# Two heads per transpose for the latent keys, the rope key as eight fp32 products, and a reordered opening

## The reference

```python
def mla_expand(c_kv, k_rope, w_kvup, qk_k_norm):
    kv = (c_kv @ w_kvup).reshape(B, K, 8, 64 + 64)          # 8 heads: 64 plain key dims, 64 value dims
    k_nope, v = kv[..., :64], kv[..., 64:]
    kr = jnp.broadcast_to(k_rope[:, :, None, :], (B, K, 8, 32))   # 32 rope dims, shared by the heads
    return rmsnorm(jnp.concatenate([k_nope, kr], axis=-1), qk_k_norm), v
# in a layer
h = rmsnorm(x, norm_mix); proj = h @ w_in                   # q latent 384, kv latent 256, rope key 32, ...
c_kv = rmsnorm(kv_lat, mla_kv_norm); k_rope = apply_rope(kr_raw, pos)
km, vm = mla_expand(concat(past latents, c_kv), concat(past rope keys, k_rope), ...)
ym = mla_attend(qm, km, vm, ...)                            # chunk-causal softmax(q k / sqrt(96)) v
```

## Time and profile before

| | us |
|---|---|
| median of 3 runs | 1072.66 (1070.98 to 1074.01) |
| the profiled execution | 1072.71 |
| its span | 1070.9 |

### The profile page before, as it was taken

How to read it: one execution, slowest core, us unless ns; L and a number is a source line. 1 busy time by engine, 2 the same in 40 slices (tenths; PEclk the granted TensorE clock), 3 DMA queues, 4 the chain that set the end, 5 groups by cost and what they waited for, 6 DMA issues and landing times.

```text
span 1070.9 us, 19944 instructions
## 1 busy us (share of the span) xinstructions
PE 1056.9 (99%) x7558; PEld 1020.8 (95%) x7558; DVE 632.9 (59%) x1047; ACT 507.0 (47%) x895; POOL 312.7 (29%) x230
## 2 busy tenths in 40 slices
PE   8899999999999999999999999999999999999998
PEld 6889988999999999999989999889999999999998
DVE  5659655445666665643566795544457666556444
ACT  6455745444454434334454466444445443443332
POOL 1655454651121111100124645565312111110000
PEclk9999999999999999999999999999999999999999
DMA  6446333324444444445413444332345354444443
GB/s 229 117 119 180 125 117 101 110 92 152 142 136 159 159 153 151 143 162 168 158 65 135 137 131 125 118 101 96 121 146 167 115 168 151 156 139 155 158 142 123
DMA packets 48769, 147.90 MB, mean 138 GB/s; under 512 B 8480, under 2 KB 13952, under 8 KB 48704
## 3 DMA queue, kind: packets, MB, share of 16 engines
q1 hardware_dynamic: 41552, 142.79, 41.5%
q10 hardware_dynamic: 7152, 4.20, 1.3%
HBM read 143.75 MB, written 3.22 MB: 137 GB/s over the span
## 4 chain that ended last, share of the span: by engine, by line
PE 93%; DVE 4%; ACT 1%; POOL 1%; issue 0%; ACTq 0%; POOLq 0%; DVEq 0%
PE psum L479 28%; PE psum L480 27%; PE psum L481 27%; PE psum L642 1%; PE psum L603 1%; PE psum L634 1%; PE psum L626 1%; PE psum L567 1%; POOL ssum L1731 1%; PE psum L570 1%; PE psum L568 1%; PE psum L587 1%; PE psum L588 1%; PE psum L674 0%; PE psum L590 0%; PE psum L846 0%
## 5 line engine op out<-in xcount | busy, mean ns | idle before, releaser
L479 PE MATMUL psum<-AH,WH 128*128 128x320 f32 x1344 | 421.1, 313 | 1.2 <-DVE krt L1537 0.7
L481 PE MATMUL psum<-AH,WL 128*128 128x320 f32 x1344 | 415.3, 309 | 0.0
L480 PE MATMUL psum<-AL,WH 128*128 128x320 f32 x1344 | 415.2, 309 | 0.0
L479 PEld LDWEIGHTS psum<-AH,WH 128*128 128x128 f32 x1344 | 252.3, 188 | 6.5 <-issue 4.2
L480 PEld LDWEIGHTS psum<-AL,WH 128*128 128x128 f32 x1344 | 252.4, 188 | 0.9
L481 PEld LDWEIGHTS psum<-AH,WL 128*128 128x128 f32 x1344 | 252.3, 188 | 0.0
L922 ACT CAST WH<-raw 128x1024 fp32r<-128x1024 f32 x175 | 182.6, 1046 | 138.5 <-PE psum L481 136.8
L1736 POOL TENSOR_TENSOR WL<-raw,WH 128x1024 fp32r<-128x1024 f32 x71 | 174.0, 2461 | 167.1 <-ACT WH L922 167.1
L1305 DVE TENSOR_TENSOR WL<-raw,WH 128x1024 fp32r<-128x1024 f32 x102 | 126.3, 1239 | 116.9 <-ACT WH L922 116.7
L1490 DVE TENSOR_TENSOR WL<-raw,WH 128x1024 fp32r<-128x1024 f32 x88 | 107.6, 1223 | 49.6 <-ACT WH L1073 48.2
L1741 POOL TENSOR_TENSOR fab<-fa,fb 128x320 f32<-128x320 f32 x44 | 38.7, 879 | 270.1 <-DVE fb L1495 270.1
(11 more groups left out here) (239 smaller groups left out, 1556.7 us busy)
## 6 DMA issues: line engine op xcount, KB each, us to landing
raw<-w_all SPq DMA_DIRECT2D x267, 512.0 KB, 3.5
y_out<-X SPq DMA_DIRECT2D x8, 160.0 KB, 3.0
ckv<-lat_in ACTq DMA_DIRECT2D x2, 384.0 KB, 5.4
X<-x_in ACTq DMA_DIRECT2D x2, 320.0 KB, 8.5
X<-x_in ACTq DMA_DIRECT2D x1, 640.0 KB, 10.4
lat_out<-ckv ACTq DMA_DIRECT2D x2, 320.0 KB, 4.3
scratch<-brel SPq DMA_DIRECT2D x8, 63.8 KB, 4.1
bias<-scratch SPq DMA_DIRECT2D x8, 48.0 KB, 4.2
```

The lines of the kernel that those rows point to most:

```text
L479: mm(out, WH[:, slot, c0:c0 + cols], high, start=first, stop=False)
L480: mm(out, WH[:, slot, c0:c0 + cols], low, start=False, stop=False)
L481: return mm(out, WL[:, slot, c0:c0 + cols], high, start=False, stop=last)
```

## The change

1. `Kn` holds all plain columns (8 x 64) first and then all rope columns (8 x 32). A block is turned in six transposes: four of two heads each, two of four heads' rope rows each. `key_columns` moves them in three instructions per engine (plain rows of the even heads and rope rows of two groups on ScalarE, the rest on VectorE), and both `kt_act` and `kt_dve` are awaited before the first transpose of the next block.
2. The rope key is computed by eight fp32 matmuls of 64 weight columns, straight from x and a weight scaled by the norm's gain on VectorE (`WF`), even chunks into PSUM rows 0 to 63 and odd chunks into 64 to 127. ScalarE copies one half out (`rope_half`), VectorE adds the two and scales.
3. The first key and value products wait for the high half alone, the last two matmuls of the group for the low one.
4. Opening: `WARM` 7; the first weight unit is loaded in two halves by two engines; the table load stands ahead of the last four of ScalarE's loads; in layer 0 ScalarE rounds the first latent unit ahead of the key blocks, casts two chunks of x already between the first block's key square and its value copy, and the second latent unit in block 2; the unit `U_KR` isn't rounded any more, and `U_QL`, `U_QL + 1` and `U_QL + 2` each come one place earlier; GpSimd splits its unit and sums the first squares earlier.
5. The splits of the units `U_QL + 1`, `U_QL + 2` and `U_POOL` go from GpSimd to VectorE. `low(l, U_KR)` on VectorE gives way to `WF`. In layer 0 the latent's sum goes into the middle of the unit `U_QL + 1`.
6. `prompt()` of item 5 is issued before the values of item 4, `sample()` after them.

```diff
-WARM = 4
+WARM = 7
...
+    rW = base[0]
     WH = sb("WH", [128, RING, 1024], F32R)
+    WF = at("WF", [128, KC, 64], F32, rW + U_KR % RING * 4096)
...
-        sp.dma_start(raw[:, 0, :], w_all[stored(0)]).then_inc(raw_ready[0], 16)
+        sp.dma_start(raw[:, 0, 0:512], w_all[stored(0)][:, 0:512]).then_inc(raw_ready[0], 16)
...
+        def rope_columns(l):
+
+            open_tile(l, T_KR)
+            pe.wait_ge(s.split_ready, l * NU + U_KR + 1)
+            for k in range(KC):
+                half = slice(k % 2 * 64, k % 2 * 64 + 64)
+                last = mm(psum[half, tbank(T_KR), 0:T], WF[:, k, :], X[:, k, :], start=k < 2, stop=k >= KC - 2)
+            last.then_inc(s.tile_full, 1)
...
             if kb == 0:
-                pe.wait_ge(s.split_ready, l * NU + U_KVK + 1)
+                pe.wait_ge(s.high_ready, l * NU + U_KVK + 1)
...
+            if kb == 0:
+                pe.wait_ge(s.split_ready, l * NU + U_KVK + 1)
             for c in range(2):
                 last = mm(out, ckvH[:, c, keys], wl[:, c], start=False, stop=c == 1)
             last.then_inc(s.kn_full, 1)
...
-            for h in range(MH):
-                if kb > 0 and h % 4 == 0:
-                    if h == 0:
-                        pe.wait_ge(s.kt_act, l * KB + kb)
-                    else:
-                        pe.wait_ge(s.kt_dve, l * KB + kb)
-                last = nc.tensor.transpose(psum[0:QK, h // 4, (h % 4) * 128:(h % 4) * 128 + 128],
-                                           Kn[:, kb % 2, h, :], ident)
-                if h % 4 == 3:
+            if kb > 0:
+                pe.wait_ge(s.kt_act, l * KB + kb)
+                pe.wait_ge(s.kt_dve, l * KB + kb)
+            for c in range(6):
+                last = nc.tensor.transpose(psum[:, c // 4, (c % 4) * 128:(c % 4) * 128 + 128],
+                                           Kn[:, kb % 2, c * 128:c * 128 + 128], ident)
+                if c in (3, 5):
                     last.then_inc(s.kt_full, 1)
...
             if i == SW_ITEMS:
-                prompt()
+                if part == 0:
+                    prompt()
+                    return
                 pe.wait_ge(s.tile_free, l * NT + item_tile(SW_ITEMS - 1) + 1)
                 last = sample()
...
-            dense(l, U_KR, T_KR)
+            rope_columns(l)
...
-                if i + 1 < SW_ITEMS:
-                    scores(l, i + 1)
+                scores(l, i + 1)
                 values(l, i)
 
             for j in range(4):
                 i = SW_ITEMS + j
-                scores(l, i)
+                scores(l, i, part=1)
...
+        def rope_half(l):
+
+            act.wait_ge(s.tile_full, l * NT + T_KR + 1)
+            nc.scalar.copy(krt[64:128, 1, :], psum[0:64, tbank(T_KR), 0:T]).then_inc(s.kr_half, 1)
...
+        def cached_first(l):
 
             lat = lat_in[ds(l, 1)].rearrange("a p c n -> (a p) c n")
             act.dma_start(ckv[:, :, T:T + 128], lat[:, :, 0:128]).then_inc(s.cache_lat[0], 16)
+            if l == 0:
+                act.dma_start(raw[:, 0, 512:1024], w_all[stored(0)][:, 512:1024]).then_inc(s.half_in, 16)
             act.dma_start(krT[64:96, T:NKEY], kr_in[ds(l, 1)].rearrange("a p n -> (a p) n")).then_inc(s.cache_kr, 16)
+
+        def cached_rest(l):
+
+            lat = lat_in[ds(l, 1)].rearrange("a p c n -> (a p) c n")
             act.dma_start(ckv[:, :, T + 128:NKEY], lat[:, :, 128:PAST]).then_inc(s.cache_lat[1], 16)
...
-            A(Kt[0:QK, 0:4, KEY0[kb]:KEY0[kb] + n],
-              psum[0:QK, 0, :].rearrange("p (h n) -> p h n", h=4)[:, :, 0:n], ACT.Copy,
-              scale=kgain[0:QK]).then_inc(s.kt_act, 1)
+            keys = slice(KEY0[kb], KEY0[kb] + n)
+            A(Kt[0:NOPE, 0:MH:2, keys], psum[0:64, 0, :].rearrange("p (h n) -> p h n", h=4)[:, :, 0:n], ACT.Copy,
+              scale=kgain[0:64, 0:1])
+            act.wait_ge(s.kt_full, 2 * (l * KB + kb) + 2)
+            for r in range(2):
+                rows = slice(r * 32, r * 32 + 32)
+                ins = A(Kt[NOPE:QK, r:MH:4, keys], psum[rows, 1, 0:256].rearrange("p (h n) -> p h n", h=2)[:, :, 0:n],
+                        ACT.Copy, scale=kgain[rows, 1:2])
+            ins.then_inc(s.kt_act, 1)
...
-        cached_latent(0)
+        cached_first(0)
+        act.wait_ge(s.warm_zero, 1)
+        A(small[:, 31:32], ssum[:, 0:1], ACT.Sqrt)
+        cached_rest(0)
         act.dma_start(X[:, 0:2, :], x_in[:, 0:2, :]).then_inc(s.x_in[0], 16)
         act.dma_start(X[:, 2:4, :], x_in[:, 2:4, :]).then_inc(s.x_in[1], 16)
         act.dma_start(X[:, 4:8, :], x_in[:, 4:8, :]).then_inc(s.x_in[2], 16)
-        act.wait_ge(s.warm_zero, 1)
-        A(small[:, 31:32], ssum[:, 0:1], ACT.Sqrt)
         cached_high(0, 0)
+        act.wait_ge(s.half_in, 16)
         high(0, U_KVK)
         high(0, U_KVV)
         cached_high(0, 1)
+        high(0, U_KV)
...
+            keys = slice(KEY0[kb], KEY0[kb] + n)
+            dve.wait_ge(s.kt_full, 2 * (l * KB + kb) + 1)
+            v.tensor_scalar(Kt[0:NOPE, 1:MH:2, keys], psum[64:128, 0, :].rearrange("p (h n) -> p h n", h=4)[:, :, 0:n],
+                            kgain[64:128, 0:1], None, ALU.mult)
             dve.wait_ge(s.kt_full, 2 * (l * KB + kb) + 2)
-            v.tensor_scalar(Kt[0:QK, 4:8, KEY0[kb]:KEY0[kb] + n],
-                            psum[0:QK, 1, :].rearrange("p (h n) -> p h n", h=4)[:, :, 0:n],
-                            kgain[0:QK], None, ALU.mult).then_inc(s.kt_dve, 1)
+            for r in range(2, 4):
+                rows = slice(r * 32, r * 32 + 32)
+                ins = v.tensor_scalar(Kt[NOPE:QK, r:MH:4, keys],
+                                      psum[rows, 1, 0:256].rearrange("p (h n) -> p h n", h=2)[:, :, 0:n],
+                                      kgain[rows, 1:2], None, ALU.mult)
+            ins.then_inc(s.kt_dve, 1)
 
...
-            low(l, U_KR)
+            dve.wait_ge(raw_ready[U_KR % RING], (l * (NU // RING) + U_KR // RING + 1) * 16)
+            TT(WF[:], raw[:, U_KR % RING, :].rearrange("p (k c) -> p k c", k=KC)[:, :, 0:64],
+               col(C_MIX, l, n=KC)[:, :, None].to_broadcast([128, KC, 64]), ALU.mult).then_inc(s.split_ready, 1)
             low(l, U_QL)
+            low(l, U_QL + 1)
             stream_rstd(l, 0)
             scaled(l, T_KV, kvr[:, 0, :])
             scaled(l, T_KV + 1, kvr[:, 1, :])
+            low(l, U_QL + 2)
 
             dve.wait_ge(s.cst_in, 32)
 
             p = full_tile(l, T_KR)
-            TT(krt[64:128, 0, :], p[64:128, 0:T], rstd[64:128], ALU.mult).then_inc(s.tile_free, 1)
+            dve.wait_ge(s.kr_half, l + 1)
+            TT(krt[64:128, 0, :], p[64:128, 0:T], krt[64:128, 1, :], ALU.add).then_inc(s.tile_free, 1)
             dve.wait_ge(s.tile_free, l * NT + T_KR + 1)
+            link(l, TT(krt[64:128, 0, :], krt[64:128, 0, :], rstd[64:128], ALU.mult))
             TT(krt[64:96, 1, :], krt[64:96, 0, :], tab[64:96], ALU.mult)
             link(l, TT(krt[64:96, 2, :], krt[96:128, 0, :], tab[96:128], ALU.mult))
             TT(krT[64:96, 0:T], krt[64:96, 1, :], krt[64:96, 2, :], ALU.add).then_inc(s.kr_ready, 1)
             scaled(l, T_QL, qlr[:, 0, :])
-            if l == 0:
-                scaled(l, T_QL + 1, qlr[:, 1, :])
             r = recip(l, N_KV, 128, T)
             STT(ckv[:, 0, 0:T], kvr[:, 0, :], col(C_MKV, l), r, ALU.mult, ALU.mult)
             STT(ckv[:, 1, 0:T], kvr[:, 1, :], col(C_MKV + 1, l), r, ALU.mult, ALU.mult).then_inc(s.stat_applied, 1)
-            if l > 0:
-                scaled(l, T_QL + 1, qlr[:, 1, :])
+            scaled(l, T_QL + 1, qlr[:, 1, :])
             dve.wait_ge(s.ckv_high, l + 1)
             TT(ckvL[:, :, 0:T], ckv[:, :, 0:T], ckvH[:, :, 0:T].bitcast(F32), ALU.subtract).then_inc(s.ckv_ready, 1)
+            low(l, U_POOL)
```

More of the change, by code:

```diff
@@ L497, in dense, with latent_sum @@
             for k in range(KC):
+                if k == KC // 2 and between is not None:
+                    between()
                 last = products(out, u % RING, k * 128, 128, AH[:, k, :], AL[:, k, :], k == 0, k == KC - 1)
             last.then_inc(s.tile_full, 1)
+        def latent_sum(l):
+            b = stat_bank(l, N_KV + 1)
+            pe.wait_ge(s.sq_kv, l + 1)
+            for m in range(2):
+                last = mm(psum[:, b, 0:T], ones, SQ[:, m, :], start=m == 0, stop=m == 1)
+            last.then_inc(s.stat_full, 1)
         def two_dense(l, u, banks, ah, al, ready, value, done, between=None, cuts=(0, KC - 1, KC),
@@ L1117, in _ @@
             if l == 0:
-                for k in range(4):
-                    norm_chunk(l, 0, k, high=False)
                 act.wait_ge(s.x_in[2], 16)
@@ L1508, in _ @@
             dve.wait_ge(s.par_in, 16)
[L1509 removed]
+            dims, turn = slice(0, NOPE), slice(NOPE, QK)
+            for c in range(2):
+                TT(kgain[c * 64:c * 64 + 64, 0:1], col(C_GK, l, dims), col(C_GQ, l, dims), ALU.mult)
+            for r in range(4):
```

(2 more changed lines are left out.)

97 lines of the change are left out of this document (51 added, 46 removed).

## The result

| | us | ratio to before (95%) |
|---|---|---|
| before, median of 15 runs | 1072.67 (1070.79 to 1075.61) | |
| after, median of 15 runs | 1075.82 (1074.43 to 1077.36) | 1.0032 (1.0024 to 1.0039) |

The change costs 3.4 us by the ratio (3.2 by the medians), where 5.4 us of gain were forecast. The profiled execution of the changed kernel took 1077.36 us for a span of 1075.6: it is the longest of the 15, with a mean clock of 0.995.

The account below looks back on a forecast made before the run. TensorE was taken as the bound, busy 1056.9 of 1070.9 us. Layer 0 at -6.2, layer 1 at +0.3 and the scores at +0.5 summed to -5.4, so 1067.3 us, with a range of 1062.3 to 1071.0.

Parts of the forecast that it names:

- Layer 0, opening: Layer 0's start: TensorE starts at 7.9 us, first transposes at 15.8 against 16.42; layer 0 in all -6.2 us.
- the third rival: TensorE's clock falls after waits: one to three falls give 1069.0 to 1072.4 us, from the fourth 1074.1; chance 0.15.
- the doubled gains ... cost nothing beyond this walk: All layers: moved splits, doubled gains and divided first load add no time beyond the steps already priced.
- The key columns: Key blocks: three instructions per engine instead of one cost VectorE 0.95 us more per block, ScalarE about 0.75.
- the walk of layer 1: Layer 1's key blocks along VectorE: latent products end 2.1 us later; with rope and later blocks, +0.3 us.
- The rope key: Rope key in both layers: eight fp32 matmuls on column halves take 2.4 us instead of 3.60, 1.2 less per layer.
- "Layer 0", from the rope products to the new keys: Layer 0's middle: rope products end at 36.4 us, new keys start at 50.0 instead of 54.27, without a slow stretch.
- Prompt scores ahead: Last window item: a wait of 0.85 us becomes 1.1 before the sample scores; +0.3 per layer, +0.5 in all.
- its first rival: VectorE's key column price is hidden: layer 1 gives -2.8 us, the opening 1.3 more, 1062.9 us; chance 0.25.

Follow-up runs that it names:

- old_loads: Changed kernel with the opening's loads in the order of the kernel before (first weight unit whole, table load last): 1072.39 us, ratio 0.9996.
- eight_keys: Changed kernel with the eight transposes, one key column instruction per engine and single gain of before: 1067.10 us, ratio 0.9948.
- longer_warm: Changed kernel with ten warm matmuls instead of seven: 1074.90 us, ratio 1.0020.
- gains_early: Changed kernel with layer 0's six gains computed earlier, before VectorE's split of the remaining latents: 1073.81 us, ratio 1.0006.
- loads_and_gains: Changed kernel with the edits of both old_loads and gains_early: 1071.58 us, ratio 0.9992.
- eight_old_loads: Changed kernel with the eight transposes, key columns and single gain of before, and the opening's loads as before: 1064.71 us, ratio 0.9924.
- three_on_vector: eight_old_loads with VectorE's 96x512 key columns cut into 64x512 and two of 32x256: 1068.28 us, ratio 0.9956.
- three_on_scalar: eight_old_loads with ScalarE's 96x512 key columns cut into three pieces, VectorE's left whole: 1066.57 us, ratio 0.9938.
- middle_only: Kernel before with only the halved rope key, the splits moved to VectorE with their casts, and the moved latent sum: 1066.80 us, ratio 0.9947.
- rope_only: Kernel before with only the rope key on column halves: 1075.86 us, ratio 1.0024.
- one_split_on_gpsimd: eight_old_loads with the split of the third query unit back on GpSimd in both layers: 1063.60 us, ratio 0.9917.

## Why the prediction was wrong

**The failed step: "Layer 0, opening", to the first transposes.** The forecast had TensorE start at 7.9, the remaining latents at 10 and the first transposes at 15.8. They came at 9.60, 12.53 and 19.91. I put the lateness of that load down to its issue, "some 1.9 us later", 1.28 of it for the table load, "behind another 256 KB". The 8.52 of the earlier trace rows and 1.9 are 10.4 already, so the 10 left nothing for the 256 KB. The trace has it the other way round. The issue came only 0.58 us later, about the length of the one more issue, with the table load beside it, and the time from issue to landing grew from 6.4 to 9.8 us. It was 8.0 to 9.8 in the five traces with the new loads and 6.3 to 7.5 in the fifteen with the old ones. What in the new order slows the transfer stays open: the half unit now stands ahead of the latents in ScalarE's issues, and no run takes it back alone. Behind the load come ScalarE's moved cast and the first square, at 14.21 instead of my 11.75. old_loads puts 3.9 us on all this. The small load of the first latents, issued at 0.74 as before, is no such case. Its cast came at 7.72 here but at 5.03 in eight_keys with the same loads, against 5.74 to 6.99 in the traces with the kernel before's opening. The prediction had named loads after 11 us as what would make it wrong.

The clock fell three times up to the new keys of the profiled execution, twice before, as the third rival said; in the median it weighs little. The ground against that rival, that only waits over 2.5 us were followed by a fall, does not hold in this trace: one fall came behind a wait of 2.07 and one behind three short ones, while a wait of 2.44 in longer_warm had none.

**"... the doubled gains ... cost nothing beyond this walk"** is the second failed statement. Two operands in SBUF, a GpSimd split beside them, and one gain of 0.15 us took 2.27, with the first reduction behind it. That is 2.8 us in gains_early (1.4 by the trace of the changed kernel), and 0.4 with the old loads, which isn't told from nothing.

**"The key columns" and the walk of layer 1: right in kind, too small.** 1.24 us more per block on VectorE instead of 0.95 (I had bounds of 0.65 and 1.45). TensorE's waits were 1.43, 1.76 and 0.58 for my 0.9, 1.8 and 0.4; the latent products of layer 1 ended 2.8 us late instead of 2.1, and the later blocks gave 0.17 back instead of 0.6, since the next set waited for VectorE again. In layer 0 I had the period at 4.4 and then let the stream's second half end where it did; the trace adds 1.4 us of waits for low halves that VectorE makes after the late columns. Three of these four took 1.12 to 1.17 us instead of 0.54, beside GpSimd's additions for the sum of squares, which the walk had at nothing too:

```profile
34.51 3.75 DVE L1371 SCALAR_TENSOR_TENSOR AL<-X,par,AH 128x320 fp32r<-128x320 f32 x4
```

In all the six transposes cost 7.3 us (loads_and_gains against eight_old_loads), about 4.8 of it before layer 1 starts (540.27 against 535.43; of this, 0.6 is there at the first transposes already, 16.45 against 15.81). three_on_vector and three_on_scalar are 3.4 and 1.5: they don't add up to it. What is left, 2.4 us and what TensorE saves in the transposes, may be the 0.24 per block and the rule that the first transpose waits for both engines, where before the first four needed ScalarE alone; this is argued, and the two were not separated.

**"The rope key": right on TensorE** (2.31 us from start to start for my 2.4), and worth about 1.4 in the end for the 2.4 of both layers: in layer 0 VectorE sets the start of the new keys.

**"Layer 0", from the rope products to the new keys: right.** 15.9 us forecast, 42.22 to 58.18 measured, no clock of 0.50 behind the wait of 0.58. middle_only shows this alone: 5.7 us faster than before. I didn't see why it works. I priced the moved splits as time on GpSimd and VectorE, and rope_only shows that leaving them makes VectorE wait.

**"Prompt scores ahead", +0.5:** the wait of 0.83 is gone and one of 1.05 stands before the sample scores, as forecast; the sum can't be told from nothing.

The four differences, in the order before, middle_only, eight_old_loads, loads_and_gains, changed kernel: -5.7 for the middle, -2.5 for the rest of the opening and the scores (intervals that overlap by a hair), +7.3 for the six transposes, +4.3 for loads and gains. As a chain from the one kernel to the other they must add up to the measured +3.4, so the sum is no check; each difference is one measurement. By an estimate from its own terms the forecast had the six transposes at 1.6 (4.4 for VectorE's work by its first rival, less 2.8 saved), loads and gains at nothing, and so the first two at -7.0 together. The side was wrong because late loads and held gains in the opening were priced at a part or at zero, and because the cost of a VectorE that is already full was carried through in layer 1 and dropped on the way in layer 0.

## What to carry to other kernels

Fewer instructions on the bound engine are worth nothing when an engine that paces it gets more of them: lengthen its chain in every stage, not only in the one where you saw it full. Dividing and moving loads to have one part sooner can make another part later: the remaining latents landed at 10.6 us or later in all five traces with the new loads, and before 9.7 in the fifteen with the old ones. Look at the time from issue to landing of each, in more than one execution. And before a VectorE instruction with two operands in SBUF is moved or added, see what GpSimd does at that moment, and the other way round.

## What the runs showed of the hardware

A VectorE instruction with two operands in SBUF that starts while a GpSimd split (two SBUF operands, 2.4 us) is under way ends with it or up to 0.4 us behind it. A gain of 0.15 took 2.27 to 2.36 us (five kernels); rope steps of 0.48 or 0.49 that began in the first half microsecond of a split took 2.44 to 2.74, and two that began 0.4 before its end 0.72 and 0.74 (rope_only, one_split_on_gpsimd). An instruction with an operand in PSUM (0.49) and a reciprocal of 320 columns (2.15) took their usual time when they began inside a split. The trace of before has held ones too: its first latent scaling took 1.55 us beside a split, the second 0.54. GpSimd is held in the same way: an addition of 0.88 took 1.66 beside VectorE's splits and 4.63 beside five VectorE instructions in a row. The Trainium skill, SBUF — State Buffer, "SBUF: two separate sides", says that VectorE with two SBUF inputs and GpSimd share a pair of ports as an "exclusive lock, not a bandwidth split", which whichever starts first keeps for the whole instruction. The held VectorE rows agree. The addition of 4.63 does not fit "whichever starts first": its record starts 0.52 us before VectorE's split, which was not held (1.21 us). Starts on GpSimd are rough in these records, so this stays open.

A short piece is dear: a 32x256 key column of VectorE, a quarter of the area of a 64x512, takes 0.48 us against 0.76, on ScalarE 0.47 against 0.67.
